# Block products in the embedding gates of a two-block decoder kernel: seven products of half the depth in place of eight, put together on VectorE

## What is computed

```
u2 = rms_norm(h, norm_ffn_g[i])
...
h = h + f
e = rms_norm(p[i] @ ple_proj[i], ple_norm_g[i])
h = h + jax.nn.sigmoid(h @ ple_gate[i]) * e
```

## Time and profile before

| | us |
|---|---|
| median of three runs | 3236.71 |
| lowest, highest | 3236.35, 3239.36 |
| profiled execution | 3235.86 |
| its span, first to last instruction | 3234.0 |
| TensorE matmul busy in it | 3157.3 |
| VectorE busy | 1392.8 |
| ScalarE busy | 807.6 |
| GpSimd busy | 169.0 |

### The profile page before, as it was taken

One profiled execution on the slowest core, in us unless ns is written; L12 is line 12 of the kernel. 1 busy time (PEld: TensorE's weight loads), 2 busy tenths in 40 slices (PEclk: granted clock), 3 DMA queues, 4 the chain that ended last, 5 costly groups with the idle time before them and its releaser, 6 DMA issues. The chain is left out here.

```text
span 3234.0 us, 46425 instructions
## 1 busy us (share of the span) xinstructions
PE 3157.3 (98%) x18957; PEld 1845.5 (57%) x18957; DVE 1392.8 (43%) x2513; ACT 807.6 (25%) x2139; POOL 169.0 (5%) x157
## 2 busy tenths in 40 slices
PE   8999999999999999999999999999999999999999
PEld 7845686685568567785684586864333333333333
DVE  7743386775447545633575336432112111212122
ACT  4413343351234243221352233232100000000000
POOL 0001000000000002300001104010100000000000
PEclk9999999999999999999999999999999999999999
DMA  7542045344424440134344511142899999899993
GB/s 292 195 157 105 27 160 218 131 172 161 163 75 166 182 177 27 66 115 153 153 172 153 188 56 65 54 179 87 347 382 401 393 399 399 342 393 400 392 401 134
DMA packets 81042, 665.51 MB, mean 206 GB/s; under 512 B 10528, under 2 KB 11168, under 8 KB 14016
## 3 DMA queue, kind: packets, MB, share of 16 engines
q1 hardware_dynamic: 80400, 661.31, 52.5%
q10 hardware_dynamic: 432, 1.24, 0.1%
HBM read 661.46 MB, written 1.05 MB: 205 GB/s over the span
## 5 line engine op out<-in xcount | busy, mean ns | idle before, releaser
L4078 PE MATMUL psum<-ring,arena 128*32 128x512 f32 x5376 | 587.8, 593 | 0.0
L878 PE MATMUL psum<-ring,arena 128*128 128x256 f32 x1760 | 398.4, 379 | 2.0 <-DVE arena L977 1.1
L4078 PEld LDWEIGHTS psum<-ring,arena 128*32 128x32 f32 x5376 | 172.3, 110 | 389.6 <-issue 388.7
L878 PEld LDWEIGHTS psum<-ring,arena 128*128 128x128 f32 x1760 | 333.8, 190 | 48.9 <-DVE ring L990 3.1
L878 PE MATMUL psum<-ring,xT_norm 128*128 128x256 f32 x1320 | 305.0, 381 | 8.9 <-DVE arena L1044 7.3
L4110 PE MATMUL psum<-ring,arena 128*32 128x512 f32 x2688 | 293.6, 592 | 0.7 <-DVE arena L4246 0.7
L878 PEld LDWEIGHTS psum<-ring,xT_norm 128*128 128x128 f32 x1320 | 251.1, 191 | 45.2 <-issue 9.2
L931 ACT ACTIVATE arena<-arena 32x128 f32<-32x128 f32 x880 | 269.5, 306 | 27.3 <-DVE arena L1065 17.7
L990 DVE TENSOR_TENSOR ring<-ring 128x1024 f32<-128x1024 f32 x220 | 266.8, 1215 | 13.2 <-DMA ring<-in_ffn_w 6.8
L4242 DVE TENSOR_TENSOR arena<-arena,psum 128x256 f32<-128x256 f32 x84 | 35.5, 423 | 411.0 <-ACT arena L4216 411.0
L898 PE MATMUL psum<-ring,arena 128*128 128x512 f32 x440 | 205.8, 592 | 0.0
(11 more groups left out here) (594 smaller groups left out, 3504.0 us busy)
## 6 DMA issues: line engine op xcount, KB each, us to landing
ring<-in_moe_w SPq DMA_DIRECT2D x340, 1024.0 KB, 7.2
ring<-in_ffn_w SPq DMA_DIRECT2D x50, 2048.0 KB, 7.6
ring<-in_ffn_w SPq DMA_DIRECT2D x65, 1024.0 KB, 4.9
ring<-in_merge_w SPq DMA_DIRECT2D x16, 2048.0 KB, 8.3
ring<-in_feat_w SPq DMA_DIRECT2D x12, 2048.0 KB, 8.7
ring<-in_ev_in_w SPq DMA_DIRECT2D x4, 2048.0 KB, 9.0
ring<-in_od_in_w SPq DMA_DIRECT2D x4, 2048.0 KB, 9.4
ring<-in_merge_w SPq DMA_DIRECT2D x8, 1024.0 KB, 11.6
```

Source lines behind the costliest of these rows:

```text
L878: last = pe.matmul(psum[:, bank, 0:GROUP], a[:, k, :], w[:, k, :], start=(fresh and k == 0), stop=(k == KT // 2 - 1), skip_group_check=True)
L4078: last = pe.matmul(psum[part(j), r, :], xg[:, u.i, u.group // GROUPS, r * P + BLOCK * j:r * P + BLOCK * (j + 1)], m[:, j, :], start=(u.i = ...
```

## The change

The gates of one layer are a product of two 2 x 2 block matrices: rows of `h` (b = 0, 1) by halves of the depth (`k` 0 to 3 and 4 to 7), and halves of the depth by column halves. Before, each of the four output blocks takes two block products, eight in all. Now seven products P1 to P7 are made, each of four matmuls of 128x512 into a bank, out of blocks and of sums of blocks:

- `mix_on_vector` makes S1 to S4 from blocks of `prog.xT`, 4 slices of 128 x 128 each;
- `sum_on_vector` makes T1 to T4 from blocks of the weights, 4 x 512 elements in each partition. T3 overwrites the block 12, which no product reads itself;
- results: (0, 0) = P1 + P2; u2 = P1 + P6; v = u2 + P7; (1, 1) = v + P5; (1, 0) = v - P4; (0, 1) = u2 + P5 + P3, where P3 is accumulated onto P5 in its bank, and waits until VectorE has taken P5 for (1, 1) (`gate_sum`, 2).

ScalarE copies P1 out of PSUM. VectorE puts the four tiles together into `gates` in SBUF, in the order (0, 0), (1, 1), (1, 0), (0, 1) of (b, c), and the sigmoid works in place there. The buffers for S, T, p1, u2 and v lie in the arena, in the first phase from its start, in the last behind what the phase holds already.

```diff
--- before.py
+++ after.py
@@ -1143,6 +1143,64 @@
 
     z = prog.const("zero")
     return z.bitcast(BF16).unsqueeze(1).to_broadcast([P, 2, 2 * P])
+
+
+BLOCK_PRODUCTS = ("P1", "P2", "P5", "P6", "P3", "P7", "P4")
+BLOCK_FACTORS = {"P1": ("11", "11"), "P2": ("12", "21"), "P3": ("S4", "22"), "P4": ("22", "T4"),
+                 "P5": ("S1", "T1"), "P6": ("S2", "T2"), "P7": ("S3", "T3")}
+
+
+class SevenProducts:
+
+
+    def __init__(self, prog, ph, weights, lhsT, banks, mem, order=BLOCK_PRODUCTS):
+        self.prog, self.weights, self.banks, self.order = prog, weights, banks, order
+        low, high, half = slice(0, KT // 2), slice(KT // 2, KT), KT // 2
+        w = [weights.buffer(c).rearrange("p (k n) -> p k n", k=KT) for c in range(2)]
+        self.w = {"11": w[0][:, low], "21": w[0][:, high], "12": w[1][:, low], "22": w[1][:, high], "T3": w[1][:, low]}
+        for name in ("T1", "T2", "T4"):
+            self.w[name] = mem.take(half, BANK)
+        self.a = {"11": lhsT[:, low, 0:P], "12": lhsT[:, high, 0:P], "21": lhsT[:, low, P:S], "22": lhsT[:, high, P:S]}
+        for i in range(4):
+            self.a[f"S{i + 1}"] = mem.take(half, P)
+        self.mixed, self.summed, self.made = (ph.semaphore(n) for n in ("rows_mixed", "weights_summed", "blocks_made"))
+
+    def bank(self, name):
+        return self.prog.psum[:, self.banks[name], :]
+
+    def wait_made(self, eng, name):
+        eng.wait_ge(self.made, self.order.index(name) + 1)
+
+    def mix_on_vector(self, dve, i):
+        out, a, b, op = (("S1", "21", "22", ALU.add), ("S2", "S1", "11", ALU.subtract),
+                         ("S4", "12", "S2", ALU.subtract), ("S3", "11", "21", ALU.subtract))[i]
+        if i in (1, 2):
+            dve.wait_ge(self.mixed, i)
+        dve.tensor_tensor(self.a[out], self.a[a], self.a[b], op).then_inc(self.mixed, 1)
+
+    def sum_on_vector(self, dve, i):
+        out, a, b = (("T1", "12", "11"), ("T2", "22", "T1"), ("T3", "22", "12"), ("T4", "T2", "21"))[i]
+        if i == 0:
+            self.weights.wait(dve, 0)
+            self.weights.wait(dve, 1)
+        elif i in (1, 3):
+            dve.wait_ge(self.summed, i)
+        dve.tensor_tensor(self.w[out], self.w[a], self.w[b], ALU.subtract).then_inc(self.summed, 1)
+
+    def on_tensor(self, pe, name, wait_rows=None, fresh=True):
+        left, right = BLOCK_FACTORS[name]
+        if left[0] == "S":
+            pe.wait_ge(self.mixed, {"S1": 1, "S2": 2, "S4": 3, "S3": 4}[left])
+        if right[0] == "T":
+            pe.wait_ge(self.summed, int(right[1]))
+        else:
+            self.weights.wait(pe, int(right[1]) - 1)
+        for k in range(KT // 2):
+            if wait_rows:
+                wait_rows(k)
+            last = pe.matmul(self.bank(name), self.a[left][:, k, :], self.w[right][:, k, :], start=(fresh and k == 0), stop=(k == KT // 2 - 1),
+                             skip_group_check=not fresh)
+        last.then_inc(self.made, 1)
 
 
 def add_projection(prog, weights, sources, lhsT, junk, gain):
@@ -4425,55 +4483,93 @@
             pool.tensor_tensor(self.e[:, b, :], self.e[:, b, :], self.gain, ALU.mult).then_inc(self.scaled, 1)
         pool.wait_ge(self.scaled, 2 * TB)
 
-    def add(self, weights, gates, junk, last, entered=False):
+    def add(self, weights, gates, junk, last, entered, mem):
         prog, e = self.prog, self.e
+        p1, u2, v = (mem.take(BANK) for _ in range(3))
         with prog.phase() as ph:
-            bank_full, squashed, weighted = (ph.semaphore(n) for n in ("bank_full", "squashed", "weighted"))
-            order = [(c, b) for c in range(2) for b in range(TB)]
+            p1_copied, mixes, gate_sum, squashed, weighted = (
+                ph.semaphore(n) for n in ("p1_copied", "u2_and_v", "gate_sum", "squashed", "weighted"))
+            order = [(0, 0), (1, 1), (1, 0), (0, 1)]
             head = Entry(prog, ph, None, None, (6, 7), norm=False) if entered else Head(prog, ph, None, None, scaled=False)
-            tail = Tail(prog, ph, junk, [(b, c) for c, b in order])
+            tail = Tail(prog, ph, junk, order)
+            seven = SevenProducts(prog, ph, weights, prog.xT, {"P1": 0, "P2": 1, "P5": 2, "P6": 3, "P7": 4, "P4": 5, "P3": 2}, mem, FIRST_PRODUCTS)
+            tile = lambda b, n: gates[:, b, n * BANK:(n + 1) * BANK]
 
             @ph.block.tensor
             def _(pe):
                 head.on_tensor(pe)
-                for n, (c, b) in enumerate(order):
-                    weights.wait(pe, c)
-                    w = weights.buffer(c).rearrange("p (k n) -> p k n", k=KT)
-                    for k in range(KT):
-                        if n == 0 and not entered:
-                            head.wait_k(pe, k)
-                        elif n == 1 and entered and k % 4 == 0:
-                            head.wait_block(pe, (1, k // 4))
-                        last_mm = pe.matmul(prog.psum[:, n, :], prog.xT[:, k, b * P:(b + 1) * P], w[:, k, :],
-                                            start=(k == 0), stop=(k == KT - 1))
-                    last_mm.then_inc(bank_full, 1)
+                for name in FIRST_PRODUCTS:
+                    first = {"P1": 0, "P2": KT // 2}.get(name)
+                    if name == "P3":
+                        pe.wait_ge(gate_sum, 2)
+                    elif name in ("P7", "P4") and not entered:
+                        head.wait_k(pe, KT - 1)
+                    seven.on_tensor(pe, name, None if entered or first is None else lambda k: head.wait_k(pe, first + k), name != "P3")
 
             @ph.block.scalar
             def _(act):
                 if not entered:
                     head.on_scalar(act)
-                for n, (c, b) in enumerate(order):
-                    act.wait_ge(bank_full, n + 1)
-                    act.activation(gates[:, b, c * BANK:(c + 1) * BANK], prog.psum[:, n, :], ACT.Sigmoid).then_inc(squashed, 1)
+                seven.wait_made(act, "P1")
+                act.activation(p1, seven.bank("P1"), ACT.Copy).then_inc(p1_copied, 1)
+                for n, (b, c) in enumerate(order):
+                    act.wait_ge(gate_sum, n + 1)
+                    act.activation(tile(b, c), tile(b, c), ACT.Sigmoid).then_inc(squashed, 1)
                 if not last:
                     tail.on_scalar(act)
 
             @ph.block.vector
             def _(dve):
-                head.on_vector(dve)
-                for n, (c, b) in enumerate(order):
+                def weigh(n):
+                    b, c = order[n]
                     cols = slice(c * BANK, (c + 1) * BANK)
                     dve.wait_ge(squashed, n + 1)
-                    dve.tensor_tensor(e[:, b, cols], e[:, b, cols], gates[:, b, cols], ALU.mult).then_inc(weighted, 1)
+                    dve.tensor_tensor(e[:, b, cols], e[:, b, cols], tile(b, c), ALU.mult).then_inc(weighted, 1)
                     dve.wait_ge(weighted, n + 1)
                     dve.tensor_tensor(prog.x[:, b, cols], prog.x[:, b, cols], e[:, b, cols], ALU.add).then_inc(tail.added, 1)
+
+                if entered:
+                    seven.sum_on_vector(dve, 0)
+                head.on_vector(dve)
+                if entered:
+                    dve.wait_ge(head.copied, 2)
+                else:
+                    for by in range(2):
+                        dve.wait_ge(head.turned_by[by], 4)
+                seven.mix_on_vector(dve, 0)
+                if not entered:
+                    seven.sum_on_vector(dve, 0)
+                seven.mix_on_vector(dve, 1)
+                seven.sum_on_vector(dve, 1)
+                seven.mix_on_vector(dve, 2)
+                seven.mix_on_vector(dve, 3)
+                seven.sum_on_vector(dve, 2)
+                seven.sum_on_vector(dve, 3)
+                seven.wait_made(dve, "P2")
+                dve.wait_ge(p1_copied, 1)
+                dve.tensor_tensor(tile(0, 0), seven.bank("P2"), p1, ALU.add).then_inc(gate_sum, 1)
+                seven.wait_made(dve, "P6")
+                dve.tensor_tensor(u2, seven.bank("P6"), p1, ALU.add).then_inc(mixes, 1)
+                weigh(0)
+                seven.wait_made(dve, "P7")
+                dve.wait_ge(mixes, 1)
+                dve.tensor_tensor(v, seven.bank("P7"), u2, ALU.add).then_inc(mixes, 1)
+                dve.wait_ge(mixes, 2)
+                dve.tensor_tensor(tile(1, 1), seven.bank("P5"), v, ALU.add).then_inc(gate_sum, 1)
+                weigh(1)
+                seven.wait_made(dve, "P4")
+                dve.tensor_tensor(tile(1, 0), v, seven.bank("P4"), ALU.subtract).then_inc(gate_sum, 1)
+                weigh(2)
+                seven.wait_made(dve, "P3")
+                dve.tensor_tensor(tile(0, 1), u2, seven.bank("P3"), ALU.add).then_inc(gate_sum, 1)
+                weigh(3)
                 if not last:
                     tail.on_vector(dve)
 
             @ph.block.sync
             def _(sp):
                 if last:
-                    for n, (c, b) in enumerate(order):
```

(4 more changed lines are left out.)

## The result

The change made the kernel faster, by more than forecast. Thirteen runs of each had medians of 3230.34 us (3225.66 to 3235.42) and 3236.87 us (3233.65 to 3258.60); the ratio, changed by before, is 0.9962 with an interval of 0.9947 to 0.9977, that is 0.38% less where 0.17% was forecast. The ratio follows the means (3229.87 and 3241.84, 12.0 us less); the medians, which the forecast speaks of, lie 6.5 us apart, 0.20%, and the changed kernel's is 1.0 us from the forecast 3231.3. The two measures part because three of the 13 runs of before took 3253 to 3259 us and none of the changed kernel did. The profiled execution took 3230.37 us with a span of 3228.2, 5.8 us less than the span of before.

What follows compares the result with a forecast made beforehand. TensorE, busy 98% of the span, was taken to bound the kernel. Per phase -3.43 + 0.72 + 0.03 = -2.68 us, two phases -5.4, giving 3231.3 us, 0.17% less; the 8 in 10 range was 3228.8 to 3234.8.

Steps and rivals of the forecast that it cites:

- Matmuls: TensorE in each phase: 28 matmuls instead of 32, 56 records instead of 64, taking 3.43 us off the path.
- The last result: Behind each phase's last matmul: VectorE adds P3's bank to u2 before the sigmoid, 0.72 us more on the path.
- the sigmoid from SBUF: Last sigmoid of each phase, reading SBUF instead of PSUM: 0.03 us more, between bounds of 0 and 0.035.
- Sums of weights: VectorE's T1 to T4, 2048 elements each: 2.29 to 2.45 us, taken as 2.45, ready in time for TensorE.
- The spare time at P3: TensorE's wait before P3 for VectorE's (1, 1) sum: costs nothing, with 1.8 us to spare.
- Sum per phase: Net of matmuls, last sum and sigmoid in each phase: -2.68 us, -5.4 us over two phases.
- A: TensorE waits inside the phase, at P3 or a late T: 3232.6 to 3236.7 us, middle 3234; chance 0.09.
- C: Sums of weights at half rate if GpSimd runs beside VectorE, 5.47 us a T: 3249.5 us; chance 0.03.
- Rival B: TensorE's clock behind the first phase returns sooner or later: 3229.7 or 3232.9 us; chance 0.04 on either side.
- What follows: Work behind each phase: table load, squares, root and store chains stay the same, weight loads keep their distance, nothing is late.
- How the numbers follow: Chances and ranges for the whole run: forecast 0.80, scatter from three runs of before, 2.7 us above the median, 0.4 below.

Runs made afterwards that it cites:

- e4: Changed kernel with P2 computed last, added onto P1 in its bank, so the last tile needs no sum: phases 31.32 and 28.06 us, ratio to before 0.9973.
- e5: Changed kernel with six unused 512-element VectorE additions ahead of the sum v in both phases: phases 34.20 and 30.94 us, one run 3232.0 us.
- e6: Changed kernel with eight 1024-element GpSimd additions beside the last phase: that phase 39.32 us, one run 3248.6 us.
- e7: Changed kernel with 24 matmuls of zeros on TensorE behind P3 in the first phase: mean 3234.6 us, ratio to before 0.9977.
- e2: Kernel before with seven products in the first phase only: phases 32.07 and 31.50 us, ratio to before 0.9986.
- e8: Changed kernel with P2 computed last and 24 matmuls of zeros behind the first phase's products: mean 3229.5 us, ratio to before 0.9954.
- e11: Kernel before with three of the last tile's matmuls left out in the first phase: that phase 32.11 us, ratio to before 0.9983.
- e13: Changed kernel with 6 matmuls of zeros ahead of P3 in the first phase: that phase 33.36 us, ratio to before 0.9977.
- e3: Kernel before with seven products in the last phase only: phases 34.68 and 28.81 us, ratio to before 1.0001.
- e10: Changed kernel with 12 matmuls of zeros ahead of P3 in the first phase: that phase 34.65 us, ratio to before 0.9999.
- e9: Changed kernel measured again without any edit: ratio to before 0.9972 (0.9953 to 0.9990).
- e1: Kernel before, unedited, measured against itself: ratio 1.0008 (0.9981 to 1.0035).
- e12: Kernel before with 12 matmuls of zeros ahead of the last tile's in the first phase: that phase 37.26 us, ratio to before 1.0006.

## Why the prediction was right, and where it was wrong

- *Matmuls*, -3.43 us a phase: right. 56 records in 24.05 us.
- *The last result*, +0.72, and *the sigmoid from SBUF*, +0.03: right, 0.70 and 0.03 in the chain, 0.75 together by e4. All eight sigmoids from SBUF take 629 to 631 ns and all eight from PSUM 597, so the step is 0.032 us; the estimate from the Trainium skill ("VectorE: DVE Perf Modes", section on the TRN2 errata), 0.043, has its sign and is 0.011 too large.
- *Sums of weights*: 2.29 us each, the lower of my two bounds; I had taken 2.45. Nothing hung on it. The spare time at P3 was foreseen as 1.8 us; in the trace it is 1.82 in the first phase.
- *Sum per phase*, -2.68: 2.62 and 2.67 measured. The first phase is 0.06 short of it, at its end: from VectorE's reciprocal (L599) to SyncE's next issue it takes 0.41 us where it took 0.34. The phase has more semaphores than before; that this is the reason was not tried.
- *Rivals A and C*: not met, but both mechanisms exist (e5, e6). A's spare time and C's condition were judged right; C's price was not (see e6).
- *Rival B*: the clock stayed low for 3.3 us into the work, in before too (I had read 3.1), so neither side came. The price I gave, half of 3.1 us at most, has its measure in e7: 1.27 us. How fast the clock comes back does differ a little between profiles: in the 13 that have that pause, the 16 transposes behind it took 3.29 to 3.68 us.

The step that failed is the last of *What follows* ("nothing is late next") together with *How the numbers follow*: I took everything outside the two phases to move by 2.7 us and to be otherwise the same, so the rest of the program stands in the sum with nothing, and the scatter was taken from three runs of before, 2.7 us at most. What the runs showed in its place: 26 of 134 runs of before are long, by some 20 us, and with a first phase shorter by 1.3 to 3.4 us it is 1 of 94 (e2, e4, e7, e8, e11, e13 and the change), against 32 of 158 where the length is as before (before, e3, e10). In the first comparison, which gave the ratio of 0.9962, the mean fell by 12.0 us: 5.3 are the two phases, 4.4 the three long runs of before, and 2.3 are left with an uncertainty of 2.3. The median, which three long runs of 13 hardly move, came out near the forecast; that is no merit of the forecast, which didn't know of them.

Over all runs the mean fell by 11.3 us, 0.35%: 5.3 for the phases, 3.9 for the long runs, 2.1 left. But the others among the runs of before differ from one comparison to the next (3237.5 to 3239.7 us on average). Against those beside it e9 has 1.0 left (uncertainty 2.4), and e1, which has no edit at all, 2.0 (3.0). So no saving beyond phases and long runs is shown. The scatter that covers it goes with the clock: runs of before that aren't long have mean clocks of 0.990 to 0.994, and average 3243 us at the one end and 3232 at the other.

Shown, by 32 of 158 against 1 of 94, is that kernels with the shorter first phase have almost no long runs; that it is the length and not the products rests on e10 and, less firmly, on e11. That the long stretch in the recurrence is what all long runs have in common is inferred from the one that was profiled. Why an earlier start makes it rare is open. The place in time counted from the start of the program can hardly be it, since the first phase, and all behind it, shifts by up to 12.3 us from one execution to another anyway.

## What to carry to other kernels

Work taken out of a phase bound by TensorE comes off the time one for one, less what is put behind the last matmul; before settling the order of partial results, look for the one whose tile needs no sum afterwards, and compute it last. Ask of each new wait how early its producer is, in microseconds, and of each new VectorE instruction whether GpSimd runs beside it. And judge a change of a few microseconds by the length of its stage in the trace; the total of a few runs can be moved by the clock of a stage far ahead or far behind, and a shift alone can go with that. Say also whether a ratio is of means or of medians: here they gave 12.0 and 6.5 us for the same 26 runs.

## What the runs showed of the hardware

- TensorE's granted clock can fall to 0.50 in a stretch where it is hardly idle, and stay there while it works: in e3's profile for over 36 us of recurrence with small matmuls, behind a single pause of 1.01 us. A pause of 2.46 us close to the same place (e12), and one of 1.74 us (e7), left it at 1.00. Whether it falls in such a stretch differs from execution to execution of one program: the mean clock of an early stage of 80 us was 0.96 in one profile and 0.82 in another, with the same code.
- Long runs were 32 of 158 with the first phase as long as before, and 1 of 94 with it 1.3 to 3.4 us shorter. The one that was profiled has its low clock some 270 us behind that phase.
- Over a pause of 6.9 us the clock fell in the changed kernel; filling 5.3 us of it with matmuls of zeros kept it at 1.00 (e7), and was worth 1.27 us.
- Beside GpSimd's additions of 1024 elements, a VectorE addition of 512 elements went from 0.69 to 2.38 us and one of 2048 from 2.29 to 3.98: in both cases 1.69 us more (e6). GpSimd's own took 1.89 to 3.82 us there.
